# Tile order of one norm, one norm in place, and the order of GpSimd's subtractions in the last expert blocks

## The chip, the cores and the metric

The kernel runs on one core of one Trainium2 chip. The metric is the device time of one execution in microseconds. The engines are named as in the profile: PE (TensorE), DVE (VectorE), ACT (ScalarE), POOL (GpSimd), and SP, whose queue issues the loads.

## The reference

Two networks of two layers each run one after the other on 256 tokens of width 1024 (the first one also carries 256 context tokens as a second sequence). What matters here:

```python
# first network, per layer
h = _ffn_half(h, ...)                       # both sequences
u = _modnorm(h, g, shift, scale)            # h * rsqrt(mean(h*h) + eps) * g, scaled and shifted
y = _fourier_mixer(u, w)                    # layer 0
y, _ = _retention_mixer(u, uc, w_in, ...)   # layer 1: q, k, v, g = split(u @ w_in)
h = h + gate * y
h = _ffn_half(h, ...)
...
x = _rmsnorm(h, final_norm_g)               # ends the first network, is the second one's input

# second network, per layer
u = rmsnorm(x, ln1_w[l]);  proj = u @ w_in[l]   # then three attention branches, merged
x = x + merged @ w_out[l]
x = x + peer_ffn(rmsnorm(x, ln2_w[l]), ...)     # 16384 experts, 128 x 128, gates mostly zero
return rmsnorm(x, lnf_w)
```

In retention q is needed for the 256 tokens of the first sequence only, k and v for both.

## The kernel before

**Layout.** Activations lie by feature: x holds 8 tiles (KD) of 128 features by 512 tokens, the first sequence in columns 0 to 255, the second in 256 to 511. Weights come as a stream of blocks of 1 MB (16 tiles of 128 x 128) through a ring of four slots; SP issues the load of block b when block b-4 is done (`block_done`).

**A product in three parts.** Each weight is split into a rounded part and a rest, and each activation likewise, and PE does rounded x rounded, rounded x rest and rest x rounded. For each half of a block (8 tiles) ACT writes the rounded part into one of two buffers (`round`, line 241; `round_next`, line 3205), and POOL then writes the rest, block minus rounded part, over the ring's slot (`leave_rest`, line 269). A buffer for half h of block b can be rounded again when PE is done with that half of block b-2. PE waits for `rest_done[h]` before half h.

**Stages.** Each engine runs a list of stages in order, each engine with a program of its own; `stage_done` counts finished stages, and finer semaphores join engines inside a stage.

**Norm.** ACT squares the 8 tiles (line 637), PE sums them over features and spreads the inverse root over partitions, DVE scales tiles of 128 x 256 (line 715). Where the next stage multiplies, ACT rounds each scaled tile (line 657) and DVE writes its rest (line 705), which raises `input_split`. With two sequences the 16 tiles come in the order (feature tile 0, sequence 0), (0, 1), (1, 0), ... With `early` set, ACT squares a tile as soon as the stage before has finished it; otherwise it waits for `stage_done`. While the norm runs, ACT also rounds the first two blocks of the next stage.

**Retention** begins with four blocks of 256 columns for q (two halves each, banks 0 to 3, 256 tokens), then k, v, and the gate. Half 0 of block 0 goes along with the norm, tile by tile:

```python
                    if j == 0 and e == 0:
                        self.input_tile(pe, k)     # waits for both sequences' tile k
```

Half 1 of block 0 and blocks 1 to 3 follow. ACT's part of the stage first waits for `stage_done` of the norm, issues a load (line 1257), and then, for each block, rounds the block two ahead (which waits for PE to be done with the present one) and copies q out of PSUM.

**Between the networks** a norm with the final gain writes to another place in SBUF (B_U), and the stage `Replace` copies it into x with one DVE instruction (line 3301). Then the norm of the second network's first layer waits for the whole of it, and ProjectIn follows.

**PeerExperts** runs over 128 expert blocks: 108 in a loop, and 20 "held" ones whose hidden values were worked out earlier. These go in ten pairs, each pair one weight block: half e of block n + p holds the output weights of expert 2p + e. For product (p, e) DVE multiplies the held values by the gates (line 3252), ACT writes the rounded part (line 3192) after PE is done with product (p-1, e), then rounds half e of the pair's next block but for the first one, and DVE writes the rest (line 3254). POOL's order is

```python
        for j in range(n, self.blocks):
            self.leave_rest(j, 0, self.split_count(j))
            self.leave_rest(j - 1, 1, self.split_count(j - 1))
```

while ACT rounds (n+1, 1), (n+2, 0), (n+2, 1), (n+3, 0), ...

Of the kernel before, what the change touches and what calls it, by code (L numbers as in the profile page):

```python
# [16 lines left out]
N = 256  # L17
KD = D // P
# [170 lines left out]
class Stage:  # L189
# [88 lines left out]
    def dve(self, dve, link):  # L278
        pass
# [298 lines left out]
class Norm(Stage):  # L578
# [7 lines left out]
    def __init__(self, chip, out, sq, small, tokens, bank, mod=None, gain=None, parts=None, kept=None, tables=None, mods=None,  # L586
                 lead=None, slots=(4, 5, 6)):
        super().__init__(chip)
# [14 lines left out]
        self.spread = chip.signals("inverse_spread", 1)  # L603
        self.tiles = [(d, s) for d in range(KD) for s in range(tokens // N)]
        self.scaled = chip.signals("scaled", len(self.tiles))
        self.rounded = chip.signals("input_rounded", len(self.tiles) if parts else 0)
        self.input_split = chip.signals("input_split", len(self.tiles) if parts else 0)
# [11 lines left out]
    def act(self, act, link):  # L619
        c, nc = self.chip, self.nc  # L620
        early = isinstance(self.before, (Project, PeerExperts))
        spare = columns(c.vec, "spare")
# [5 lines left out]
        if self.first_mods:  # L628
            lead = self.first_mods
# [104 lines left out]

def first_norm(chip, tokens, mod, mods, split=True, lead=None):
    small = [chip.at(A_SMALL + i * 2 * N, 2 * N)[:, 0:tokens] for i in range(2)]
    sq = chip.at(A_SQ if tokens == 2 * N else R_P, KD, tokens)
    return Norm(chip, chip.at(A_U, KD, 2 * N)[:, :, 0:tokens], sq, small,
                tokens, 7, mod=mod, parts=first_input(chip, tokens) if split else None, mods=mods, lead=lead)

# [309 lines left out]
class Retention(Stage):  # L1050
# [73 lines left out]
    def pe(self, pe):  # L1124
        nc, ps = self.nc, self.chip.ps

        def columns_of(j, out, tokens):

            whi, wlo = self.weights(j)
            for e in range(2):  # L1130
                pe.wait_ge(self.chip.rest_done[e], self.split_count(j))
                for k in range(KD):
                    i = e * KD + k
                    if j == 0 and e == 0:
                        self.input_tile(pe, k)
                    last = self.product(out(e), (whi[:, i, :], wlo[:, i, :]),
                                        (self.u[0][:, k, 0:tokens], self.u[1][:, k, 0:tokens]), k == 0, k == KD - 1)
            last.then_inc(self.chip.block_done, 1)

        for j in range(4):  # L1140
            columns_of(j, lambda e: ps[:, j, e * N:(e + 1) * N], N)
        pe.wait_ge(self.chip.cst1_loaded, 32)

# [1899 lines left out]
class PeerExperts(Stage):  # L3043
# [164 lines left out]
    def pool(self, pool, link):  # L3208
# [5 lines left out]
        with pool.Fori(1, n // RING) as it:  # L3214
            for r in range(RING):
                b = it * RING + r
                self.leave_rest(r, 0, self.split_count(b))
                self.leave_rest((r - 1) % RING, 1, self.split_count(b - 1))
        for j in range(n, self.blocks):
            self.leave_rest(j, 0, self.split_count(j))  # L3220
            self.leave_rest(j - 1, 1, self.split_count(j - 1))
        self.leave_rest(self.blocks - 1, 1, self.split_count(self.blocks - 1))

# [56 lines left out]
def second_network(chip, start):  # L3280
    vec = chip.vec[:]

    stages = [second_norm(chip, columns(vec, "final_g")), Replace(chip)]
    for layer in range(DEPTH):
# [8 lines left out]
    return stages + [final, Finish(chip, final.u)]  # L3293


class Replace(Stage):


    def dve(self, dve, link):
        dve.wait_ge(self.chip.stage_done, self.index)  # L3300
        self.nc.vector.tensor_copy(self.chip.x[:, :, 0:N], self.chip.at(B_U, KD, N)).then_inc(self.chip.stage_done, 1)

# [74 lines left out]
def first_network(chip, start):  # L3377
# [3 lines left out]
    for layer in range(DEPTH):  # L3381
# [4 lines left out]
                               table=dft if first else None)  # L3386
        stages.append(first_norm(chip, 2 * N, 1, mods, split=layer > 0))
        if layer == 0:
# [249 lines left out]
```

## Time and profile before

| | |
|---|---|
| runs | 4486.83, 4493.26 and 4490.0 us; median 4490.0 us |
| profiled execution | 4486.41 us, of which the profile's span is 4484.6 us |
| PE busy | 4287.9 us (96% of the span) |
| POOL busy | 2612.0 us (58%) |
| DVE busy | 1874.5 us (42%) |
| ACT busy | 1863.9 us (42%) |
| mean granted TensorE clock | 0.982 of full speed |

Busy time of PE is no measure of how well it is used, since matmuls are pipelined; the idle times before its instructions and the granted clock tell more. In a timeline a row is: start in us, duration in us, engine, line, operation, what it writes and reads, count, and in brackets the idle time before it with what ended it. Several instructions in a row are merged, with the duration of all of them.

### The profile page before, as it was taken

The numbers are of one execution on the slowest core, as the hardware profiler recorded it, in microseconds if no ns is written. First come the engines' busy times: TensorE is split into PE (matmuls) and PEld (weight loads), VectorE is DVE, ScalarE is ACT, GpSimd is POOL, SyncE is SP. The second block draws the span as 40 slices with busy tenths as digits, with TensorE's granted clock in tenths as the row PEclk, the third lists the DMA queues.
The fourth block names the chain that finished last, engine by engine and source line by source line (L and its number), as shares of the span: only waits on it lengthen the run. The fifth ranks groups of instructions, "written<-read, shape, count | busy, mean of one in ns | idle before, by whom it ended". The sixth has DMA issues, their size and how long they took to land.

```text
span 4484.6 us, 62631 instructions
## 1 busy us (share of the span) xinstructions
PE 4287.9 (96%) x24214; PEld 3670.8 (82%) x24214; DVE 1874.5 (42%) x3572; ACT 1863.9 (42%) x3030; POOL 2612.0 (58%) x1270
## 2 busy tenths in 40 slices
PE   7999999999999999899999999999989999999998
PEld 5787787878878999877897888887868897888886
DVE  5741377032022422554578222223555487222223
ACT  4433343232233444452334555554451424555554
POOL 3443244444444478630467888887720567888886
PEclk9999999999999999999999999999999999999999
DMA  7643367222222245440242455555530351555554
GB/s 264 217 160 94 100 224 273 94 85 99 99 104 94 85 161 187 165 146 34 87 168 71 159 188 187 187 188 207 174 135 20 113 174 39 188 188 188 188 188 160
DMA packets 109503, 659.23 MB, mean 147 GB/s; under 512 B 11504, under 2 KB 17904, under 8 KB 40048
## 3 DMA queue, kind: packets, MB, share of 16 engines
q1 hardware_dynamic: 99072, 637.22, 40.3%
q10 hardware_dynamic: 10224, 19.11, 1.6%
q8 instruction: 148, 2.42, 0.2%
q14 instruction: 59, 0.48, 0.0%
HBM read 646.84 MB, written 9.44 MB: 146 GB/s over the span
## 4 chain that ended last, share of the span: by engine, by line
PE 86%; DVE 6%; ACT 3%; POOL 2%; DMA 1%; issue 1%; SPq 0%; ACTq 0%; DVEq 0%; POOLq 0%
PE ps L3116 15%; PE ps L253 14%; PE ps L255 13%; PE ps L254 13%; PE ps L3106 9%; PE ps L3107 4%; PE ps L3026 3%; PE ps L2822 3%; PE ps L1664 2%; POOL ring_rest L269 2%; DVE arena L2520 1%; ACT rounded L241 1%; PE ps L2189 1%; PE ps L2207 1%; PE ps L1205 1%
## 5 line engine op out<-in xcount | busy, mean ns | idle before, releaser
L269 POOL TENSOR_TENSOR ring_rest<-ring,rounded 128x1024 fp32r<-128x1024 f32 x948 | 2317.6, 2458 | 1324.2 <-ACT rounded L241 1124.3
L253 PE MATMUL ps<-part,rounded 128*128 128x512 f32 (+1 forms) x3360 | 1150.5, 342 | 34.4 <-DVE part L705 21.5
L254 PE MATMUL ps<-part,rounded 128*128 128x512 f32 (+1 forms) x3360 | 1141.7, 340 | 0.0
L255 PE MATMUL ps<-part,ring_rest 128*128 128x512 f32 (+1 forms) x3360 | 1141.4, 340 | 0.0
L241 ACT ACTIVATE rounded<-ring 128x1024 fp32r<-128x1024 f32 x484 | 485.1, 1051 | 651.1 <-PE ps L255 641.5
L253 PEld LDWEIGHTS ps<-part,rounded 128*128 128x128 f32 x3360 | 646.1, 192 | 119.7 <-DVE part L705 21.6
L254 PEld LDWEIGHTS ps<-part,rounded 128*128 128x128 f32 x3360 | 646.5, 192 | 66.9
L255 PEld LDWEIGHTS ps<-part,ring_rest 128*128 128x128 f32 x3360 | 645.6, 192 | 67.4
L3205 ACT ACTIVATE rounded<-ring 128x1024 fp32r<-128x1024 f32 x464 | 490.2, 1056 | 333.0 <-DMA ring<-in_weights 330.8
L3106 PE MATMUL ps<-x_parts,rounded 128*128 128x512 f32 x1728 | 616.9, 397 | 1.5 <-ACTq L3040 1.5
L3116 PE MATMUL ps<-rounded,part 128*128 128x512 f32 x2048 | 592.4, 393 | 16.8 <-POOL ring_rest L269 10.0
L3107 PE MATMUL ps<-x_parts,ring_rest 128*128 128x256 f32 x1728 | 484.7, 280 | 0.0
L3116 PEld LDWEIGHTS ps<-rounded,part 128*128 128x128 f32 x2048 | 369.2, 188 | 99.3 <-POOL ring_rest L269 13.4
L3106 PEld LDWEIGHTS ps<-x_parts,rounded 128*128 128x128 f32 x1728 | 324.7, 188 | 79.4 <-ACTq L3040 1.8
L3236 DVE TENSOR_TENSOR ps<-ps,arena 128x256 f32<-128x256 f32 x216 | 134.8, 624 | 549.4 <-ACT ps L3173 549.4
L3107 PEld LDWEIGHTS ps<-x_parts,ring_rest 128*128 128x128 f32 x1728 | 326.2, 189 | 8.2
L3116 PE MATMUL ps<-ring_rest,part 128*128 128x512 f32 x1024 | 320.7, 395 | 0.0
L443 DVE SCALAR_TENSOR_TENSOR ps<-arena,ps 128x512 f32<-128x512 f32 x392 | 269.2, 746 | 9.1 <-DMA arena<-in_mod_weights 6.9
L3116 PEld LDWEIGHTS ps<-ring_rest,part 128*128 128x128 f32 x1024 | 192.2, 188 | 47.1
L932 DVE SCALAR_TENSOR_TENSOR x<-ps,mods,x 128x256 f32<-128x256 f32 x80 | 35.8, 480 | 456.3 <-PE ps L255 456.3
L821 ACT ACTIVATE arena<-ps 128x512 f32<-128x512 f32 (+1 forms) x88 | 47.9, 544 | 401.5 <-PE ps L255 401.4
L3234 DVE TENSOR_TENSOR ps<-ps,arena 128x256 f32<-128x256 f32 x216 | 93.4, 432 | 240.1 <-ACT arena L3170 240.1
(373 smaller groups left out, 5260.3 us busy)
## 6 DMA issues: line engine op xcount, KB each, us to landing
ring<-in_weights SPq DMA_DIRECT2D x528, 1024.0 KB, 4.8
arena<-in_mod_weights SPq DMA_DIRECT2D x128, 512.0 KB, 4.3
arena<-in_mod_lead SPq DMA_DIRECT2D x8, 1024.0 KB, 18.3
held<-arena ACTq DMA_DIRECT2D x20, 256.0 KB, 5.5
arena<-held SPq DMA_DIRECT2D x20, 256.0 KB, 4.6
arena<-bias_scratch ACTq DMA_DIRECT2D x2, 2048.0 KB, 8.8
bias_scratch<-arena ACTq DMA_DIRECT2D x1, 3072.0 KB, 32.1
x<-in_x SPq DMA_DIRECT2D x1, 2048.0 KB, 9.8
```

The source lines that it names most:

```text
L241: self.nc.scalar.activation(c.rounded[:, s % ROUNDED, half], c.ring[:, slot, half], ACT.Copy)\
L253: mm(out, w[0], a[0], start=start, stop=False)
L254: mm(out, w[0], a[1], start=False, stop=False)
L255: return mm(out, w[1], a[0], start=False, stop=stop)
L269: eng.tensor_tensor(c.ring_rest[:, slot, half], c.ring[:, slot, half], c.rounded[:, (self.s0 + r) % ROUNDED, half].bitcast(F32), ALU.subtr ...
L443: v.scalar_tensor_tensor(bank, self.chunk_row(i, k), self.cond[:, k, stream:stream + 1], bank, ALU.mult, ALU.add)\
L2822: last = nc.tensor.matmul(ps[:, 4 + u % self.AHEAD_BANKS, 0:N], self.chip.ring[:, slot, e * KD + k, :], self.z_whole[:, k, :], start=k == ...
L3106: nc.tensor.matmul(c.ps[:, r % 2, :], whi[:, k, :], c.x_parts[:, k, :], start=k == 0, stop=False)
L3107: last = nc.tensor.matmul(c.ps[:, r % 2, 0:N], wlo[:, k, :], self.z[0][:, k, :], start=False, stop=k == KD - 1)
L3116: last = nc.tensor.matmul(self.out(t, i), a, w[:, i * 4 * P:(i + 1) * 4 * P], start=False, stop=end and n == 2)
L3205: self.nc.scalar.activation(c.rounded[:, (self.s0 + r) % ROUNDED, half], c.ring[:, f % RING, half], ACT.Copy)\
L3236: v.tensor_tensor(gelu, gelu, self.gates[:, :, bass.ds(b + HELD, 1)].rearrange("p t a -> p (t a)"), ALU.mult)\
```

## The change

Three things are changed.

- The norm ahead of retention takes its 16 tiles sequence by sequence (`by_stream`): the 8 tiles of the first sequence, then the 8 of the second. Retention's PE program takes half 0 of blocks 0 and 1 together along with the tiles of the first sequence, then half 1 of block 0 and of block 1, then blocks 2 and 3, and waits for the second sequence's tiles after that.
- The norm at the end of the first network writes into x. `Replace` is gone. The norm after it squares each tile as soon as it is scaled (`x_ready` of a norm is its `scaled` semaphore, and `early` holds for a norm that follows a norm).
- POOL takes the rests of the held blocks in the order in which ACT rounds the halves.

```diff
     def __init__(self, chip, out, sq, small, ..., slots=(4, 5, 6), by_stream=False):
...
         self.tiles = [(d, s) for d in range(KD) for s in range(tokens // N)]
+        if by_stream:
+            self.tiles = [(d, s) for s in range(tokens // N) for d in range(KD)]
         self.scaled = chip.signals("scaled", len(self.tiles))
+        self.x_ready = self.scaled
...
-        early = isinstance(self.before, (Project, PeerExperts))
+        early = isinstance(self.before, (Project, PeerExperts, Norm))
...
-                    if j == 0 and e == 0:
-                        self.input_tile(pe, k)
...
-        for j in range(4):
+        split = self.before.input_split
+
+        def of_query(j, e, k):
+            w, i = self.weights(j), e * KD + k
+            return self.product(ps[:, j, e * N:(e + 1) * N], [x[:, i, :] for x in w], [x[:, k, 0:N] for x in self.u],
+                                k == 0, k == KD - 1)
+
+        for k in range(KD):
+            pe.wait_ge(split.sem, split.at(k + 1))
+            for j in range(2):
+                if k == 0:
+                    pe.wait_ge(self.chip.rest_done[0], self.split_count(j))
+                of_query(j, 0, k)
+        for j in range(2):
+            pe.wait_ge(self.chip.rest_done[1], self.split_count(j))
+            for k in range(KD):
+                last = of_query(j, 1, k)
+            last.then_inc(self.chip.block_done, 1)
+        for j in range(2, 4):
             columns_of(j, lambda e: ps[:, j, e * N:(e + 1) * N], N)
+        pe.wait_ge(split.sem, split.at(2 * KD))
...
-        for j in range(n, self.blocks):
+        for j in (n, n + 1):
             self.leave_rest(j, 0, self.split_count(j))
             self.leave_rest(j - 1, 1, self.split_count(j - 1))
-        self.leave_rest(self.blocks - 1, 1, self.split_count(self.blocks - 1))
+        for j in range(n + 1, self.blocks):
+            self.leave_rest(j, 1, self.split_count(j))
+            if j + 1 < self.blocks:
+                self.leave_rest(j + 1, 0, self.split_count(j + 1))
...
-    stages = [second_norm(chip, columns(vec, "final_g")), Replace(chip)]
+    small = [chip.at(B_SMALL + i * N, N) for i in range(2)]
+    stages = [Norm(chip, chip.x[:, :, 0:N], chip.at(B_SQ, KD, N), small, N, 5, gain=columns(vec, "final_g"))]
...
-class Replace(Stage):
-    def dve(self, dve, link):
-        dve.wait_ge(self.chip.stage_done, self.index)
-        self.nc.vector.tensor_copy(self.chip.x[:, :, 0:N], self.chip.at(B_U, KD, N)).then_inc(self.chip.stage_done, 1)
...
-        stages.append(first_norm(chip, 2 * N, 1, mods, split=layer > 0))
+        stages.append(first_norm(chip, 2 * N, 1, mods, split=layer > 0, by_stream=layer > 0))
```

`first_norm` passes `by_stream` on to `Norm`.

## Rows read from the trace of the kernel before

**Rows 1.** The page, part 4: shares of the chain that ended last, by engine.
```profile
PE 86%; DVE 6%; ACT 3%; POOL 2%; DMA 1%; issue 1%; SPq 0%; ACTq 0%; DVEq 0%; POOLq 0%
```

**Rows 2.** Timeline of PE, held blocks, first and last stall (idle before, releaser in brackets).
```profile
3090.32 0.73 PE L3116 MATMUL ps<-rounded,part 128*128 128x512 f32 x2 [1.26 <-POOL ring_rest L269]
...
4455.35 0.73 PE L3116 MATMUL ps<-rounded,part 128*128 128x512 f32 x2 [1.25 <-POOL ring_rest L269]
```

**Rows 3.** Timeline of ACT, held blocks: three activation copies in a row.
```profile
3086.43 0.38 ACT L3192 ACTIVATE part<-ps 128x256 fp32r<-128x256 f32 x1 [1.39 <-PE ps L3116]
...
3089.15 0.38 ACT L3192 ACTIVATE part<-ps 128x256 fp32r<-128x256 f32 x1 [1.39 <-PE ps L3116]
...
3093.43 0.38 ACT L3192 ACTIVATE part<-ps 128x256 fp32r<-128x256 f32 x1 [2.94 <-PE ps L3116]
```

**Rows 4.** Timeline of POOL, held blocks: rests of halves, two to a row.
```profile
3085.12 5.14 POOL L269 TENSOR_TENSOR ring_rest<-ring,rounded 128x1024 fp32r<-128x1024 f32 x2 [4.06 <-ACT rounded L3205]
3090.56 4.80 POOL L269 TENSOR_TENSOR ring_rest<-ring,rounded 128x1024 fp32r<-128x1024 f32 x2 [0.30 <-ACT rounded L3205]
```

**Rows 5.** Line L269 from 3085 to 3088 us: duration ns min/median/max.
```profile
L269 POOL TENSOR_TENSOR ring_rest<-ring,rounded x2: 2412/2594/2777, 3085.1 to 3087.5; 128x1024 fp32r<-128x1024 f32 x2
```

**Rows 6.** Timeline of DVE, held blocks: a multiply by the gates.
```profile
3087.19 0.84 DVE L3252 TENSOR_TENSOR ps<-arena 128x256 f32<-128x256 f32 x1
```

**Rows 7.** Timeline of DVE, final norm of the first network and what follows.
```profile
1811.73 3.22 DVE L715 SCALAR_TENSOR_TENSOR arena<-x,vec,ps 128x256 f32<-128x256 f32 x8 [0.80 <-PE ps L679]
1815.11 2.47 DVE L3301 COPY x<-arena 128x2048 f32<-128x2048 f32 x1 [0.16 <-DVEq L727]
1821.39 0.43 DVE L693 COPY arena<-ps 128x256 f32<-128x256 f32 x1 [3.82 <-PE ps L670]
```

**Rows 8.** Timeline of ACT, the same stretch.
```profile
1810.72 1.99 ACT L241 ACTIVATE rounded<-ring 128x1024 fp32r<-128x1024 f32 x2
1817.61 2.56 ACT L637 ACTIVATE arena<-x 128x256 f32<-128x256 f32 x8 [4.91 <-DVE x L3301]
```

**Rows 9.** Timeline of all engines, the same norm of the second layer.
```profile
3145.43 2.54 ACT L637 ACTIVATE arena<-x 128x256 f32<-128x256 f32 x8
...
3148.76 0.42 DVE L693 COPY arena<-ps 128x256 f32<-128x256 f32 x1 [3.37 <-PE ps L670]
```

**Rows 10.** Timeline of PE at the start of ProjectIn after the final norm.
```profile
1825.44 0.58 PE L253 MATMUL ps<-part,rounded 128*128 128x256 f32 x1 [1.69 <-DVE part L705]
```

**Rows 11.** Windows there: us, PE, PEld, DVE, ACT, POOL busy (instructions), granted clock, DMA.
```profile
1831.00:1831.50 0.50, 0.50 (x4) 0.50 (x4) 0.50 (x1) 0.00 (x0) 0.00 (x0) 0.52 1.07 389
```

**Rows 12.** Timeline of DVE, norm of retention: the first and the last rests.
```profile
1278.23 0.48 DVE L705 SCALAR_TENSOR_TENSOR part<-ps,mods,part 128x256 fp32r<-128x256 f32 x1
...
1290.07 1.26 DVE L705 SCALAR_TENSOR_TENSOR part<-ps,mods,part 128x256 fp32r<-128x256 f32 x3
```

**Rows 13.** Timeline of PE, first matmul of retention and two later ones.
```profile
1279.76 0.55 PE L253 MATMUL ps<-part,rounded 128*128 128x256 f32 x1 [2.75 <-DVE part L705]
...
1293.05 0.41 PE L254 MATMUL ps<-part,rounded 128*128 128x256 f32 x1
1293.26 0.41 PE L255 MATMUL ps<-part,ring_rest 128*128 128x256 f32 x1
```

**Rows 14.** Timeline of ACT, start of retention.
```profile
1291.42 0.34 ACTq L1257 DMA_DIRECT2D arena<-in_expo  x1
1296.82 2.01 ACT L241 ACTIVATE rounded<-ring 128x1024 fp32r<-128x1024 f32 x2 [6.15 <-PE ps L255]
...
1302.58 2.01 ACT L241 ACTIVATE rounded<-ring 128x1024 fp32r<-128x1024 f32 x2 [3.27 <-PE ps L255]
```

**Rows 15.** Timeline of POOL, norm and start of retention.
```profile
1276.61 2.35 POOL L269 TENSOR_TENSOR ring_rest<-ring,rounded 128x1024 fp32r<-128x1024 f32 x1 [0.96 <-ACT rounded L241]
1297.96 4.76 POOL L269 TENSOR_TENSOR ring_rest<-ring,rounded 128x1024 fp32r<-128x1024 f32 x2 [19.00 <-ACT rounded L241]
```

**Rows 16.** Windows of the retention stage, columns as in rows 11.
```profile
1292.00:1296.00 4.00, 4.00 (x22) 4.00 (x22) 0.00 (x0) 0.00 (x0) 0.00 (x0) 0.55 0.73 262
```

More of the change, by code:

```diff
@@ L586, in __init__ @@
     def __init__(self, chip, out, sq, small, tokens, bank, mod=None, gain=None, parts=None, kept=None, tables=None, mods=None,
-                 lead=None, slots=(4, 5, 6)):
+                 lead=None, slots=(4, 5, 6), by_stream=False):
         super().__init__(chip)
@@ L732, in first_input, with first_norm @@
     return tuple(chip.parts_at(a, KD, 2 * N)[:, :, 0:tokens] for a in (A_SQ, A_U))
-def first_norm(chip, tokens, mod, mods, split=True, lead=None):
+def first_norm(chip, tokens, mod, mods, split=True, lead=None, by_stream=False):
     small = [chip.at(A_SMALL + i * 2 * N, 2 * N)[:, 0:tokens] for i in range(2)]
@@ L738, in first_norm @@
     return Norm(chip, chip.at(A_U, KD, 2 * N)[:, :, 0:tokens], sq, small,
-                tokens, 7, mod=mod, parts=first_input(chip, tokens) if split else None, mods=mods, lead=lead)
+                tokens, 7, mod=mod, parts=first_input(chip, tokens) if split else None, mods=mods, lead=lead, by_stream=by_stream)
 class FeedForwardIn(Stage):
```

## The prediction

> **What bounds the kernel now.** I read the shares of the chain first: 86% of it is PE, so time is won only where PE stands still or runs at its lower clock [rows 1]. The change touches three places, so next came the timelines of PE, ACT, POOL and DVE there, for what ends PE's wait in each.
>
> *Held blocks* (end of each PeerExperts). A product here is PE's work on half a block, 12 matmuls. ACT's copy for a product starts when PE has finished the product two earlier, so the distance of copies is PE's pace: 3086.43 to 3089.15 is 2.72 us, and the next one 4.28 us [rows 3]. The difference, 1.56 us, is a stall of PE that POOL's rest ends; there are four in each layer, and of the eight in both the first and the last are shown [rows 2]. POOL itself is not full: it stood idle for 4.06 us before the rest that PE then waited behind, and that pair of rests ended at 3090.26, just as PE went on [rows 2, 4].
>
> *Final norm of the first network.* PE has nothing but the norms. Eight scaled tiles take 3.22 us on DVE, then comes a copy of 2.47 us, and only then eight squares on ACT; the next norm's sums are copied at 1821.39 [rows 7, 8].
>
> *Start of retention.* PE waits 2.75 us for its first tile, then does three matmuls for each two tiles of the norm, at half clock [rows 13]. The norm's last rest ends at 1290.07 + 1.26 = 1291.33 [rows 12]; the granted clock from 1292 to 1296 is 0.55, so it was 1.2 GHz until about 1295.6 and 2.4 GHz then [rows 16]. ACT rounds block 2 at 1296.82, when block 0 is done, and block 3 at 1302.58, when block 1 is done [rows 14].
>
> **Part 1, held blocks.** POOL's instructions are the same; two of each pair change places. Before, the rest of (p+1, half 0) went ahead of that of (p, half 1); but (p+1, 0) can be rounded only after PE has finished (p-1, 0), while (p, 1) was rounded earlier. POOL so stood waiting with work at hand, and PE got (p, 1) a whole rest late. After, POOL takes halves in the order in which ACT rounds them.
>
> What is late next? Take a product done at 0. ACT's copy takes 0.38, the rounding one half of 1.99, about 1.0, so POOL can begin near 1.4 [rows 3, 8]. A rest takes 2.41 to 2.78 [rows 5], so it is there by 4.3. PE needs that half as the fourth product from there, after three more: 3 x 2.72 = 8.2. That leaves 3.9 us. POOL at its slowest, 2.78 for each product against 2.72, falls behind by 0.06 x 18 = 1.1 us in a layer, less than 3.9. So no stall stays: 8 x 1.56 = 12.5 us. The lower bound lets the 1.1 us through in both layers: 10.3. I take 12.5, since the reserve is over three times the slip.
>
> The two rests of that pair differ, 2.41 and 2.78, and a DVE multiply by the gates (both inputs in SBUF), from 3087.19 to 3088.03, lies across the point where one ends and the next begins [rows 5, 6]. The Trainium skill, "SBUF — State Buffer", section "Who interferes with whom", says that a DVE instruction with two SBUF inputs and a GpSimd instruction that reads SBUF lock each other out for a whole instruction. This speaks against the change, as closer-packed rests meet every multiply: by the rule, and with the 2.78 that the trace has for a rest that met one, the 12.5 would become at worst the 10.3 above.
>
> **Part 2, final norm.** Replace and its copy go; DVE writes the scaled tiles straight into x, and the next norm's squares wait for each tile instead of the whole stage. The tiles end at 1811.73 + 3.22 = 1814.95, the last square follows after 0.03 and takes about 0.42 (2.56 for eight overlapping ones): 1815.40. ACT is no bound: it is free of rounding at 1810.72 + 1.99 = 1812.71, and eight squares from there end at 1815.27 [rows 7, 8]. From the last square to the copy of the sums is 1821.39 - (1817.61 + 2.56) = 1.22 us in the present norm; in the second layer's, where squares already follow tiles, it is 3148.76 - (3145.43 + 2.54) = 0.79 us [rows 7 to 9]. So the copy starts at 1816.19 or 1816.62, not at 1821.39: 5.2 or 4.8 us. I take 5.2, as that norm has the new shape. Nothing is queued behind the new waits of ACT but its rounding of the next block, which PE needs about 4 us later. ProjectIn then runs at half clock from 1825.44 to about 1831.3 [rows 10, 11]. This stretch may shorten: at half clock a matmul takes 0.21 instead of 0.12 us (below), so each us of it costs 0.43 us. Half of it gone would add 1.3; I put 0 and keep 1.3 for the range.
>
> **Part 3, retention.** The order of tiles costs DVE and ACT nothing: the same 16 tiles, 0.91 us each. A full block of q is 48 matmuls in 5.76 us, the distance of the roundings at 1296.82 and 1302.58: 0.12 us each; at half clock 0.21 [rows 13, 14]. The first tile's rest ends at 1278.23 + 0.48 = 1278.71 [rows 12], and PE now starts there, with six matmuls for each tile. They take 1.28 us at half clock, more than the 0.91 of a tile, so PE is dense from the start and I expect the clock back within a few us; then it follows the tiles, and the first halves of blocks 0 and 1 are done at about 1278.7 + 8 x 0.91 = 1286.0. Both second halves follow without waiting, as the last rest of block 1 ends at 1276.61 + 2.35 = 1278.96 [rows 15]: 48 x 0.12 more, blocks 0 and 1 done at about 1291.7 instead of 1302.5.
>
> Not all of these 10.8 us stay. ACT rounds block 2 only behind its wait for the whole norm. That wait still ends near 1291.42, then comes the issue of the expo load, and rounding can start at 1291.8. POOL starts 1.14 later (1296.82 to 1297.96) and a rest is half of 4.76 [rows 14, 15]: 1292.9 + 2.4 = 1295.3, and PE starts block 2 at 1295.4. So the gain is 1302.5 - 1295.4 = 7.1 us, whether blocks 0 and 1 end at 1291.7 or 3 us later. Blocks 3 and on are not late: POOL then does a rest each 2.4 us, PE uses one each 2.9.
>
> PE now stands still for 3.7 us, where before it didn't. After its wait of 2.75 us ahead of the first tile the clock was at 1.2 GHz [rows 13], so I expect that again. It costs the dense stretch at half clock: from 1291.4 to 1295.6 here, 4.2 us x 0.43 = 1.8; from 1825.44 to 1831.3, 5.9 x 0.43 = 2.5 [rows 10, 11, 16]. I take 1.8: 5.3 us stay, bounds 4.6 and 7.1, and 3.5 if PE keeps half clock all through blocks 0 and 1 (96 x 0.21 from 1278.7 is 1299).
>
> The Trainium skill, "TensorE: Matmul & The Clock Gate", section "Why this matters for your kernels", advises against idle gaps between bursts of matmuls, since the engine falls back to its lower clock. By this rule the change loses part of what it wins, 5.3 instead of 7.1, and the trace agrees with it at 1279.76.
>
> **The sum.** 12.5 + 5.2 + 5.3 = 23.0 us. The profiled execution took 4486.4 (span 4484.6 and 1.8 around it): 4463.4. The median of the three runs is 4490.0, 3.6 above it, so I say **4467**. The terms' bounds give 10.3 + 4.8 + 3.5 = 18.6 to 12.5 + 6.5 + 7.1 = 26.1, so 4464 to 4471 on the median's scale; the runs shown spread by 3.3 either way, and the likeliest case's own range is 4460 to 4475. About 0.2%, 9 us, can be told from no change.
>
> **Rivals.**
> *Held blocks keep their pace.* If POOL waits for a rounding ahead of each rest, as it does for 0.30 us ahead of some now [rows 4], a product costs 2.78 + 0.30 = 3.08; two pairs are then 12.3, against 3 x 2.72 + 4.28 = 12.4 now, and nothing is won there: 4490 - 10.5 = 4479.5. Against it: 2.78 is the slow one of the rests, and the reserve of 3.9 us has to be used up first. 0.09; half of it counts as no change, being 0.23% off.
> *Retention wins nothing*, because the gap ahead of block 2 and a clock that stays low through blocks 2 and 3 (a further 7 us) take it all: 4490 - 17.7 = 4472.3. Against it: the clock came back within 6 us of dense work in both places seen. 0.08.
> *No change to be told*: weight loads, not PE, set the pace once PE is early, and the three gains end in waits for them: 4486 to 4490. Against it: in the held blocks ACT's copies wait for PE, none for a load [rows 3]. 0.07.
> *Slower*: the held half that POOL now takes first is rounded after PE's product of that half, not before, so that each product waits for copy, rounding and rest, 4.3 us, less one product of 2.72: 1.6 us x 36 = 57, less 10.5, is 4490 + 46 = 4536. It decides once the lead of a rest falls from 8.2 to under 4.0 us (0.28 us for each product eats the other 10.5). The copies being released two products ahead speaks against it [rows 3]. 0.04.
>
> The forecast itself has 0.72. Faster: 0.72 + 0.08 + 0.05 = 0.85; no change 0.07 + 0.04 = 0.11; slower 0.04. With the first two cases, 4459 to 4477 holds about 8 in 10.
>
> **What would show it.** Held blocks: ACT's copies 2.72 us apart all through, PE with no wait for POOL. Final norm: one copy fewer on DVE, and about 4.5 us from the first scaled tile to the copy of the next sums instead of 9.7. Retention: PE starts about 1 us earlier, ends blocks 0 and 1 near the norm's last rest, then waits over 3 us for POOL's first rest of block 2, and the clock falls once more. I would be wrong if rests still end PE's waits in the held blocks, if ACT can't round block 2 by 1292, or if a later stage waits for something that didn't become earlier.

## The result

The changed kernel takes 4461.06 us (median of 4 runs, 4456.06 to 4461.67), the kernel before 4489.65 beside it (4 runs, 4486.83 to 4493.26): a ratio of 0.9934, 95% interval 0.9918 to 0.995. That is faster, by 28.6 us, and clear of the noise, where 23.0 were forecast (4467; range 4459 to 4477). The profiled executions have spans of 4484.6 and 4459.4, 25.2 us apart.

The shares of the chain, in part 4 of the profile's page of the kernel after, stand against [rows 1]: POOL has lost a point, PE and DMA have gained one each.

```profile
PE 87%; DVE 6%; ACT 3%; DMA 2%; issue 1%; POOL 1%; SPq 0%; ACTq 0%; DVEq 0%; POOLq 0%
```

**Held blocks.** PE's waits between 3050 and 3135 us of the kernel after, from the view of waits (us in total, times, longest):

```profile
PE ps L3136 <- DVE part L3262: 2.3, 1, 2.3
PE ps L673 <- ACT arena L640: 1.7, 1, 1.7
PE ps L3175 <- ACT arena L3218: 0.7, 1, 0.7
```

From its timelines of ACT, POOL and DVE, copies in a row, rests and a multiply:

```profile
3087.00 0.39 ACT L3212 ACTIVATE part<-ps 128x256 fp32r<-128x256 f32 x1 [1.39 <-PE ps L3136]
...
3089.72 0.39 ACT L3212 ACTIVATE part<-ps 128x256 fp32r<-128x256 f32 x1 [1.39 <-PE ps L3136]
...
3092.44 0.39 ACT L3212 ACTIVATE part<-ps 128x256 fp32r<-128x256 f32 x1 [1.38 <-PE ps L3136]
...
3074.81 2.40 POOL L269 TENSOR_TENSOR ring_rest<-ring,rounded 128x1024 fp32r<-128x1024 f32 x1 [2.80 <-ACT rounded L3225]
...
3088.41 2.57 POOL L269 TENSOR_TENSOR ring_rest<-ring,rounded 128x1024 fp32r<-128x1024 f32 x1 [0.20 <-ACT rounded L3225]
3091.13 30.07 POOL L269 TENSOR_TENSOR ring_rest<-ring,rounded 128x1024 fp32r<-128x1024 f32 x11 [0.16 <-ACT rounded L3225]
...
3087.76 0.95 DVE L3275 TENSOR_TENSOR ps<-arena 128x256 f32<-128x256 f32 x1
```

No line of the waits names POOL, nor does one in the second layer, where POOL ended four of PE's waits in each layer before, the first and the last of them in [rows 2] (the 2.3 us stand at the entry of these blocks, as before). From the third copy on, the copies are 2.72 us apart, where [rows 3] has 4.28 in between. POOL begins with rests of 2.40 us and idles a little before each; each rest then is longer than the one before it, and from 3091.13 on eleven stand back to back in 30.07 us, 2.73 each, just over PE's 2.72. POOL is full there now. The multiply above takes 0.95 us, where [rows 6] has 0.84, and each one is a little longer than the one before it, from 0.82 to 1.29 us in this layer.

**Final norm.** Timelines of DVE, ACT and PE of the kernel after:

```profile
1812.78 3.22 DVE L718 SCALAR_TENSOR_TENSOR x<-x,vec,ps 128x256 f32<-128x256 f32 x8 [0.80 <-PE ps L682]
1817.23 0.42 DVE L696 COPY arena<-ps 128x256 f32<-128x256 f32 x1 [1.23 <-PE ps L673]
...
1813.66 2.79 ACT L640 ACTIVATE arena<-x 128x256 f32<-128x256 f32 x8
...
1830.29 2.01 ACT L241 ACTIVATE rounded<-ring 128x1024 fp32r<-128x1024 f32 x2 [4.73 <-PE ps L255]
...
1821.27 0.39 PE L253 MATMUL ps<-part,rounded 128*128 128x256 f32 x1 [1.69 <-DVE part L708]
```

The same rounding of ACT in the kernel before:

```profile
1837.10 2.01 ACT L241 ACTIVATE rounded<-ring 128x1024 fp32r<-128x1024 f32 x2 [7.38 <-PE ps L255]
```

Windows of the kernel after there (columns as in [rows 11]):

```profile
1821.00:1823.00 2.00, 1.73 (x14) 1.73 (x15) 1.90 (x6) 1.06 (x3) 1.21 (x1) 1.00 0.00 0
1825.00:1827.00 2.00, 2.00 (x19) 2.00 (x18) 1.84 (x5) 0.39 (x1) 0.00 (x0) 1.00 0.40 99
```

The squares start 0.88 us behind the first scaled tile, with no copy between, and from that tile to the copy of the sums it is 4.45 us, where [rows 7] has 9.66: 5.2 us less. And the clock is 1.00 when ProjectIn starts, so that the first matmul takes 0.39 us where [rows 10] has 0.58. PE's first two blocks there, up to ACT's next rounding, take 9.02 us (1821.27 to 1830.29) against 11.66 (1825.44 to 1837.10): another 2.6 us.

**Retention.** Timelines of DVE, ACT, POOL and PE of the kernel after:

```profile
1294.92 1.26 DVE L708 SCALAR_TENSOR_TENSOR part<-ps,mods,part 128x256 fp32r<-128x256 f32 x3
...
1296.27 0.34 ACTq L1277 DMA_DIRECT2D arena<-in_expo  x1
1296.71 2.00 ACT L241 ACTIVATE rounded<-ring 128x1024 fp32r<-128x1024 f32 x2 [1.19 <-DVEq L727]
...
1297.84 2.35 POOL L269 TENSOR_TENSOR ring_rest<-ring,rounded 128x1024 fp32r<-128x1024 f32 x1 [14.05 <-ACT rounded L241]
...
1283.60 0.58 PE L253 MATMUL ps<-part,rounded 128*128 128x256 f32 x1 [1.75 <-DVE part L708]
...
1300.25 0.40 PE L253 MATMUL ps<-part,rounded 128*128 128x256 f32 x1 [3.46 <-POOL ring_rest L269]
```

Its windows there:

```profile
1284.00:1286.00 2.00, 2.00 (x11) 2.00 (x11) 1.93 (x6) 1.03 (x3) 0.00 (x0) 0.50 0.01 4
1288.00:1292.00 4.00, 4.00 (x36) 4.00 (x35) 3.82 (x10) 2.12 (x5) 0.00 (x0) 1.00 0.00 0
...
1300.90:1302.90 2.00, 2.00 (x11) 2.00 (x11) 0.00 (x0) 0.67 (x2) 2.00 (x2) 0.50 1.04 438
```

Everything here is 4.8 us later than before by the trace, since the start of this profile was. Less that, PE's first tile comes 1.0 us earlier than in [rows 13], the last rest of the norm is where [rows 12] has it, and ACT rounds block 2 at 1296.71, not at 1296.82 + 4.8 = 1301.6 [rows 14]. PE has blocks 0 and 1 done by then, stands still for 3.46 us until POOL's first rest of block 2 is there, and the clock, back at 1.00 by 1288, falls to 0.50 a second time.

A ledger over the whole run: how much later the same ScalarE instruction starts in each profile than in the profile of before (us from the span's start). The last column is a second profile of the kernel after.

| at us of before | what lies between | after | retention alone | norm alone | held alone | after, again |
|---|---|---|---|---|---|---|
| 1269 | start of the program | +4.83 | +7.31 | +5.12 | +5.46 | +3.60 |
| 1350 | retention's start | -0.47 | +2.91 | +5.18 | +5.28 | -1.72 |
| 1805 | rest of the first layer | +1.05 | +4.46 | +5.16 | +5.29 | -3.21 |
| 1838 | final norm, two blocks of ProjectIn | -6.81 | +3.05 | -2.71 | +5.11 | -11.09 |
| 1965 | | -8.75 | +4.51 | -4.96 | +1.07 | -13.42 |
| 3041 | | -8.98 | +4.71 | -5.18 | +6.55 | -13.14 |
| 3145 | held blocks, first layer | -13.78 | +4.81 | -3.66 | +2.03 | -19.41 |
| 3293 | | -18.89 | +4.71 | -8.37 | +1.89 | -23.56 |
| 4302 | | -18.77 | +4.88 | -8.28 | +1.84 | -23.56 |
| 4476 | held blocks, second layer | -25.24 | +4.53 | -8.46 | -4.52 | -28.53 |

Each edit takes its time off at its own place: 5.3 us at retention's start, 7.9 between 1805 and 1838, and in each layer's held blocks 6.2, since from the third of ACT's twenty copies to the eighteenth it is 46.99 us before (3083.71 to 3130.70) and 40.80 after (3076.12 to 3116.92). That makes 25.6 us with both layers. A row of the table can hold a half-clock stretch besides: 4.8 for the first layer of the kernel after, as the clock was at 0.57 from 3068 to 3072 there; 4.4 for retention alone, as the clock fell one pause of PE earlier there and the norm's first tile came 0.9 us later. The rows without an edit move by up to 5.5 us either way; the experiment on the clock's falls is about them. The first row is no loss of the change: the profile of before reaches 1269 earlier than all thirteen others, by 1.5 to 7.3 us, which is one reason why the spans differ by less than the medians.

### The profile page after: what moved, and what is told of

Same layout as the page of the kernel before. It is cut to its first block, busy times and chain, and to the rows that moved or that the text cites. A ratio compares the mean times of both kernels' runs of the same rounds, so it can differ in the third digit from the quotient of the medians.

```text
span 4459.4 us, 62630 instructions
## 1 busy us (share of the span) xinstructions
PE 4280.7 (96%) x24214; PEld 3667.2 (82%) x24214; DVE 1883.1 (42%) x3571; ACT 1864.8 (42%) x3030; POOL 2618.6 (59%) x1270
## 4 chain that ended last, share of the span: by engine, by line
PE 87%; DVE 6%; ACT 3%; DMA 2%; issue 1%; POOL 1%; SPq 0%; ACTq 0%; DVEq 0%; POOLq 0%
PE ps L3136 16%; PE ps L253 13%; PE ps L255 13%; PE ps L254 13%; PE ps L3126 9%; PE ps L3127 4%; PE ps L3046 3%; PE ps L2842 3%; PE ps L1684 2%; DVE arena L2540 1%; PE ps L2209 1%; ACT rounded L241 1%; PE ps L2227 1%; POOL ring_rest L269 1%; DMA ring<-in_weights 1%
## 5 line engine op out<-in xcount | busy, mean ns | idle before, releaser
L269 POOL TENSOR_TENSOR ring_rest<-ring,rounded 128x1024 fp32r<-128x1024 f32 x948 | 2323.7, 2466 | 1300.8 <-ACT rounded L241 1119.2
```

The costliest lines, as they stand in the source:

```text
L269: eng.tensor_tensor(c.ring_rest[:, slot, half], c.ring[:, slot, half], c.rounded[:, (self.s0 + r) % ROUNDED, half].bitcast(F32), ALU.subtr ...
```

## Experiments

**The parts one by one.** Each is the kernel before with one part of the change as it stands in the diff. *Retention alone*:

```diff
-        stages.append(first_norm(chip, 2 * N, 1, mods, split=layer > 0))
+        stages.append(first_norm(chip, 2 * N, 1, mods, split=layer > 0, by_stream=layer > 0))
...
+            for j in range(2):
...
+                of_query(j, 0, k)
```

> The kernel before with the retention part alone (norm by sequence, first two q blocks together). My theory: blocks 0 and 1 end about 10 us earlier, 3.5 us of it go to PE's wait for POOL's rest of block 2 and about 1.7 to the clock that falls in that wait, so 5.3 us stay: 4489.65 - 5.3 = 4484. From the norm's copy of sums (1273.49 before) to the end of block 3 (ACT's rounding at 1314.10 before, 40.6 us) 35.3 us. Rival (the unexplained 3 us of the whole change come from this part): 4481. Rival (the gain is given back later in the stage): 4489.

Measured: 4486.89 us against 4491.53 for the kernel before, ratio 0.9989 (0.998 to 0.9998). From the copy of sums to ACT's rounding at the end of block 3 it is 36.2 us, not 35.3, by the 0.9 us that the earlier fall of the clock cost.

*Final norm alone*:

```diff
-        early = isinstance(self.before, (Project, PeerExperts))
+        early = isinstance(self.before, (Project, PeerExperts, Norm))
...
-    stages = [second_norm(chip, columns(vec, "final_g")), Replace(chip)]
+    stages = [Norm(chip, chip.x[:, :, 0:N], chip.at(B_SQ, KD, N), small, N, 5, gain=columns(vec, "final_g"))]
```

> The kernel before with the final norm in place, Replace gone, squares per tile. My theory: from the first scaled tile to the copy of the next sums 4.45 us instead of 9.66, so 5.2 us for certain, and up to 2.6 more where ProjectIn starts at 2.4 GHz, as in the changed kernel: 4482 to 4484.5. If the clock at the start of ProjectIn belongs to the shorter idle stretch, the granted clock there is 1.0 again; the rival, that it was chance, lets it be 0.5 for some us, with 5.2 us or less won.

Measured: 4480.25, ratio 0.9975 (0.9966 to 0.9984). The clock is 1.00 again where ProjectIn starts.

*Held blocks alone*:

```diff
-        for j in range(n, self.blocks):
+        for j in (n, n + 1):
             self.leave_rest(j, 0, self.split_count(j))
             self.leave_rest(j - 1, 1, self.split_count(j - 1))
+        for j in range(n + 1, self.blocks):
+            self.leave_rest(j, 1, self.split_count(j))
+            if j + 1 < self.blocks:
+                self.leave_rest(j + 1, 0, self.split_count(j + 1))
```

> The kernel before with POOL's order in the held blocks alone. My theory: eight stalls of 1.56 us go, ACT's copies are 2.72 us apart all through, POOL's rests grow to about 2.7 us but PE never waits for them: 4489.65 - 12.4 = 4477.2. Rival (closer-packed rests are held up by the multiplies): stalls stay late in each layer, 4479.5 or more.

Measured: 4477.66, ratio 0.9966 (0.9954 to 0.9978). The copies are 2.72 us apart from the third on, in both layers.

*All three together*, beside them:

> The changed kernel once more, for a second profile. My theory: the three parts add up to 12.4 + 5.3 + 7.8 = 25.5 us, 4464; what is beyond (the median fell by 28.6) comes from stretches of lower clock elsewhere that lie differently in each execution, so a second profile has them in other places and the same three gains at the three places. Rival: the same places outside the change (around 1940 and 3270 us) are shorter by 2 to 3 us again, so that the change reaches them.

Measured: 4461.77, ratio 0.9934 (0.9921 to 0.9948). The three medians are 4.6, 11.3 and 13.9 us below before, 29.8 in all, and the whole is 29.8: the parts add up, with no sign that they hide or feed one another, though each interval is 4 us or more either way, so that the exact agreement is luck. At their places they won 4.4, 7.9 and 12.4 us. The norm's median has 3.4 us more than that. The profile of all three together has the gains at the same places (5.3, 7.9, and 6.1 and 6.4 in the two layers' rows), and around 1940 and 3270 it is again about 4 us shorter each, which is the sign that the rival named; more on that below.

**What gave ProjectIn its clock.** The kernel before, with the copy gone but the squares still behind the whole of the final norm, not tile by tile:

```diff
-    stages = [second_norm(chip, columns(vec, "final_g")), Replace(chip)]
+    stages = [Norm(chip, chip.x[:, :, 0:N], chip.at(B_SQ, KD, N), small, N, 5, gain=columns(vec, "final_g"))]
```

> The kernel before, with one half of the edit at the first network's final norm: the norm writes its result in place and the copy stage goes, but the squares are still formed behind the last residual sum, not block by block ahead of it. Theory (the 2.6 us that the change won in ProjectIn beyond my sum are the clock's: it keeps full only if PE's idle time ahead of ProjectIn is short enough): the copy's 2.5 us are won, and the clock in ProjectIn still falls to half as before, since PE's gap is only 2.5 us shorter: 4487 against 4489.65. Rival: the 2.6 us come with any shorter gap: 5 us less than before, 4484.5.

At the same place of this kernel, the timeline of ACT:

```profile
1819.93 2.56 ACT L637 ACTIVATE arena<-x 128x256 f32<-128x256 f32 x8 [2.33 <-DVEq L727]
```

The view of waits, for PE:

```profile
PE ps L670 <- ACT arena L637: 3.8, 1, 3.8
```

And windows:

```profile
1820.00:1822.00 2.00, 1.60 (x10) 0.98 (x12) 0.00 (x0) 2.00 (x7) 1.39 (x1) 0.50 0.00 0
1828.00:1830.00 2.00, 1.33 (x6) 1.34 (x7) 1.93 (x6) 1.08 (x3) 0.87 (x1) 0.50 0.00 0
```

Measured: 4483.6 against 4492.67, ratio 0.998 (0.9971 to 0.9989). The trace bears out the theory: at its place the edit won 2.6 us from the norm to ACT's rounding in ProjectIn (+4.89 to +2.31 in the ledger's measure), the copy's time and no more, and the clock was at 0.50 when ProjectIn started. (The next norm's sums are copied 2.6 us earlier; its other steps, at half clock here, take 0.9 longer, and ProjectIn's two blocks 0.9 less.) PE's idle time ahead of the squares' sums was 6.4 us before, is 3.8 here and 1.4 after. Over the 14 profiles of this study, the first matmul of ProjectIn ran at half clock in all four without early squares, and in one of the ten with them (the kernel with the early rounding, below: 0.50; in one more, the one with an extra multiply of two SBUF operands, the clock fell 1 us behind the first matmul). The median fell by 9.1 us, so 6.5 came from elsewhere; of these 4.0 us stand in its trace at 1937 to 1960 us, and they are taken up below.

**What is left in retention.** After, with block 2 rounded among the norm's tiles:

```diff
+        self.ahead = (12, 13) if by_stream else None
...
+                if self.ahead and i in self.ahead:
+                    self.next.round(act, ROUNDED, halves=(self.ahead.index(i),))
...
-            self.round(act, j + ROUNDED)
+            if j:
+                self.round(act, j + ROUNDED)
```

> The kernel after, with one thing moved: ScalarE rounds the two halves of retention block 2 among its normalized tiles (after tiles 12 and 13) and not behind the whole norm. Theory: what is left of the wait in this stage is PE's 3.5 us for GpSimd's first rest of block 2, because the rounding begins only at 1296.71, behind the last tile; begun some 2 us earlier the rest comes earlier by as much, PE waits about 1 us, and the granted clock does not fall a second time there: 2.5 to 4 us less than after, about 4457.5. Rival: the two roundings push the last three normalized tiles of ScalarE back by their 4 us, the rests of those tiles and PE's first blocks come as much later, and nothing is won: 4461, or 1 to 2 us more.

And with another order of PE's first two blocks as well (both halves of block 0 with the tiles, then block 1; rounding after tiles 10 and 11):

```diff
-            for j in range(2):
+            for e in range(2):
...
-                    pe.wait_ge(self.chip.rest_done[0], self.split_count(j))
-                of_query(j, 0, k)
+                    pe.wait_ge(self.chip.rest_done[e], self.split_count(0))
+                last = first_queries(0, e, k)
+        last.then_inc(self.chip.block_done, 1)
...
+                last = first_queries(1, e, k)
```

> The kernel after, with block 2 rounded among the tiles (after tiles 10 and 11) and PE's two blocks in another order: both halves of block 0 run with the tiles as they come, block 1 as a whole follows. Then PE has a whole block of finished operands to work on while GpSimd makes the rest of block 2. Theory (the wait for GpSimd's rest is all that is left here): the 3.5 us wait goes, and with it the clock's second fall, together 4 to 5 us less than after, about 4456. Rival: the wait only moves to block 3's rest, which GpSimd makes next, or PE's start waits for the tiles that the roundings delay: within 2 us of after, 4459 to 4463.

PE's waits in this stage that a rest of POOL ends, from the view of waits, with the early rounding:

```profile
PE ps L253 <- POOL ring_rest L269: 0.8, 1, 0.8
```

All of PE's waits in the stage with both edits, from the same view:

```profile
PE ps L253 <- DVE part L711: 1.8, 1, 1.8
PE ps L681 <- DVE arena L699: 0.9, 1, 0.9
PE ps L685 <- DVE arena L701: 0.6, 1, 0.6
```

And a window of it where the kernel after had the clock at 0.50:

```profile
1301.00:1303.00 2.00, 2.00 (x19) 2.00 (x18) 0.00 (x0) 1.01 (x2) 1.63 (x1) 1.00 0.95 291
```

Measured: 4460.12 us with the early rounding (ratio to before 0.9924, 0.9911 to 0.9937) and 4455.75 with both (0.9916, 0.9903 to 0.9929). From PE's first tile to the rounding of block 4 (24.26 us in the kernel after) the traces show 21.34 and 20.29: 2.9 and 4.0 us less. The wait shrank to 0.8 us and then went, and the clock stayed at 1.00 both times (1.00 in every window from 1291 to 1303 with the early rounding). The median of the first is only 0.9 us below the 4461.06 of the kernel after, which was not run beside it, so its 2.9 us rest on the trace; in its profile ProjectIn started at half clock and lost 2.6 us there. The second once more, beside the kernel after:

> The kernel in which both halves of retention's block 0 run with the tiles and block 2 is rounded among them, once more and now beside the kernel after. Theory: 4.0 us less than after, the difference of the two traces in this stage: 4457 against 4461. Rival: nothing is won in the end, since the clock's stretches further on give it back: 4461.

Measured: 4455.89 (ratio 0.9916, 0.9903 to 0.993) and the kernel after 4459.46 (0.9931, 0.9916 to 0.9946). That is 3.6 us less by medians. In this second profile the same stretch takes 19.12 us, 5.1 less than after, as the clock came back almost 3 us earlier than in the first one. The intervals overlap, so the gain rests on the 4.0 and 5.1 us of the two traces and on the median being lowest both times; it is the fastest kernel here.

**POOL's rests and DVE's multiplies.** After, with each held multiply done twice (the extra result goes to a spare tile):

```diff
+            v.tensor_tensor(self.low[:, e, :], h, self.gates[:, :, n], ALU.mult)
             v.tensor_tensor(self.hidden(e), h, self.gates[:, :, n], ALU.mult).then_inc(self.gated.sem, 1)
```

> The kernel after, with VectorE's multiply of a held block done twice (the first result is overwritten in place): one more operation with two SBUF inputs for each of the 18 blocks of a layer. VectorE itself has room for it. Theory: GpSimd's rest of a held block and VectorE's two-input multiply do not run side by side in full (the rests grow from 2.40 to 2.73 us where multiplies fall into them), so each rest grows by another 0.5 to 1.0 us past ScalarE's 2.72 us, GpSimd becomes the bound again, and the run takes 8 to 12 us per layer more, 17 to 24 us in all: about 4481. Rival: the rests grow for another reason (the narrow slack of their order), and the extra multiply costs nothing: 4461.

Timelines of DVE and POOL of this kernel:

```profile
3100.14 0.61 DVE L3275 TENSOR_TENSOR arena<-arena 128x256 f32<-128x256 f32 x1
...
3102.07 1.95 DVE L3275 TENSOR_TENSOR arena<-arena 128x256 f32<-128x256 f32 x1
3103.95 2.79 DVE L3276 TENSOR_TENSOR ps<-arena 128x256 f32<-128x256 f32 x1
...
3100.79 5.49 POOL L269 TENSOR_TENSOR ring_rest<-ring,rounded 128x1024 fp32r<-128x1024 f32 x2 [1.90 <-ACT rounded L3225]
```

Measured: 4497.13 against 4492.67 (ratio 1.0005, 0.9997 to 1.0014): the whole gain is gone, 36 us above the 4461 of the kernel after (32 by the two ratios to before) where 17 to 24 were expected. The direction was the theory's, but not the way in which the time is lost. Alone, at 3100.14, the multiply takes 0.61 us. Two rests stand from 3100.79 to 3106.28 and meet near 3103.53; the multiplies issued under them end at 3104.02 and 3106.74, each 0.5 us behind the end of a rest. A rest takes 2.75, hardly more than the 2.73 of the kernel after. It is DVE that waits out the whole rest, ACT's copy waits for DVE, and PE and POOL for that: the copies are 1.93 and 5.46 us apart in turn, so a product takes 3.7 us on average instead of 2.72.

Whether that is the operands or only the place of the extra work, two more kernels tell: the extra multiply in DVE's idle time behind the real one, once with both operands in SBUF and once with one in PSUM.

```diff
             v.tensor_tensor(self.hidden(e), h, self.gates[:, :, n], ALU.mult).then_inc(self.gated.sem, 1)
+            v.tensor_tensor(self.low[:, e, :], h, self.gates[:, :, n], ALU.mult)
```

> The kernel after, with one more multiply of two SBUF operands on VectorE for each held block, written to a spare tile, in VectorE's idle 1.4 us between the multiply and ScalarE's copy. Theory: such an operation waits until GpSimd's rest under way has ended and takes 0.47 us from there, so it reaches 1.3 us past the start of the subtraction behind it, and then the next block's multiply runs into the next rest: at least the 36 us of the doubled multiply, up to one whole rest per block (18 x 2.75 us in each layer, 99 us): 4497 to 4560. Rival: what cost 36 us was the extra work ahead of the multiply in VectorE's order and not its operands; put into idle time it costs nothing: 4461, and the same as the next kernel.

```diff
+            v.tensor_tensor(self.low[:, e, :], c.ps[:, e, 0:N], self.gates[:, :, n], ALU.mult)
```

> The same extra multiply at the same place, but with its first operand read from PSUM, so that only one of the two is in SBUF. Theory (two SBUF operands are what excludes GpSimd): it takes some 0.5 to 0.6 us in VectorE's idle time, GpSimd's rests stay at 2.73 us or less, and the time stays that of after: 4459 to 4465. Rival (any VectorE operation that reads or writes SBUF excludes GpSimd): the same loss as with two SBUF operands, 4497 or more.

Groups by line of the held blocks (behind the first bar the busy time and the mean ns); L3276 is the extra multiply. With two SBUF operands:

```profile
L269 POOL TENSOR_TENSOR ring_rest<-ring,rounded 128x1024 fp32r<-128x1024 f32 x17 | 46.6, 2767 | 12.4 <-ACT rounded L3225 12.4
...
L3275 DVE TENSOR_TENSOR ps<-arena 128x256 f32<-128x256 f32 x17 | 29.7, 1749 | 0.0
...
L3276 DVE TENSOR_TENSOR arena<-arena 128x256 f32<-128x256 f32 x18 | 24.2, 1344 | 0.0
```

With one operand in PSUM:

```profile
L269 POOL TENSOR_TENSOR ring_rest<-ring,rounded 128x1024 fp32r<-128x1024 f32 x17 | 46.4, 2770 | 1.9 <-ACT rounded L3225 1.9
...
L3275 DVE TENSOR_TENSOR ps<-arena 128x256 f32<-128x256 f32 x19 | 31.0, 1631 | 0.0
...
L3276 DVE TENSOR_TENSOR arena<-ps,arena 128x256 f32<-128x256 f32 x19 | 11.5, 607 | 0.0
```

Measured: 4481.87 with two SBUF operands, 4461.9 with one in PSUM, 4459.46 for the kernel after beside them. So the operands decide: the PSUM form takes 0.61 us each time, though POOL's rests run nearly without a break; the SBUF form takes 1.34 on average, 0.61 for twelve of the eighteen and 2.8 for the other six. The loss of 22 us is less than the 36 I gave as the least: I had let every block lose a rest, while POOL is idle for 12.4 us above, waiting for rounded halves, and the twelve short multiplies all began while no rest was under way.

The Trainium skill, "SBUF — State Buffer", section "Who interferes with whom", has this as a rule: a VectorE instruction with two SBUF inputs and a GpSimd instruction that reads SBUF exclude each other for a whole instruction, the one issued first holding off the other, while one with at most one SBUF input, outside the modes that use two ports, does not. The traces agree: 2.79 us against 0.61 for the same multiply.

**The clock's falls.** The kernel after once more:

> The kernel after once more, beside the three others of this call on one chip: 4461 us, as in its two earlier timings. Its profile also shows which of the half-clock stretches of TensorE come again in the same places (theory: those at 1541, 1908 and 3270 follow from the program and come again; rival: they come and go with each execution).

Windows at the same instructions, each behind PE's row at the end of the pause ahead of it, from its timeline: first the kernel after, at 1541.5 us:

```profile
1541.41 2.00 PE L1245 MATMUL ps<-arena,cst 128*128 128x256 f32 x7 [1.88 <-ACT arena L1330]
...
1541.50:1545.50 4.00, 4.00 (x17) 3.67 (x18) 1.43 (x2) 3.99 (x5) 0.44 (x1) 0.67 0.54 227
```

Its second profile, at 1540.25:

```profile
1540.16 1.99 PE L1245 MATMUL ps<-arena,cst 128*128 128x256 f32 x8 [1.88 <-ACT arena L1330]
...
1540.25:1544.25 4.00, 4.00 (x27) 3.79 (x28) 1.42 (x2) 3.99 (x5) 0.43 (x1) 1.00 0.51 217
```

The kernel before, at 1934:

```profile
1933.56 2.17 PE L2091 MATMUL ps<-arena,ring 64*128 64x256 f32 x5 [1.68 <-ACT arena L2273]
...
1934.00:1938.00 4.00, 4.00 (x15) 3.35 (x14) 0.00 (x0) 0.95 (x3) 0.00 (x0) 0.50 0.52 213
```

The kernel with the held blocks alone, whose edit comes later than this, at 1939.1:

```profile
1938.67 1.31 PE L2091 MATMUL ps<-arena,ring 64*128 64x256 f32 x5 [1.68 <-ACT arena L2273]
...
1939.10:1943.10 4.00, 4.00 (x23) 3.31 (x22) 0.73 (x2) 2.43 (x7) 0.00 (x0) 1.00 0.53 221
```

Measured: 4459.46 us. Mixed: the fall at 1541 did not come again; that named as 1908 (at 1894.5 us of the first profile) did, with 1.6 us lost in both; and around 3270 both have the same short stretch. So the rival holds at 1541, and the second pair of windows shows the same elsewhere. Ahead of the first pair PE paused for 1.88 us in both profiles, ahead of the second for 1.68 in both, and behind the same pause the clock was 0.67 in one and 1.00 in the other, 0.50 and 1.00. Such a fall costs 1.3 us at 1541 and about 4 around 1940 and 3270 each. Falls of this kind move the ledger's other rows: where one of them grows or shrinks by over 1 us, the time at half clock in it does so too.

Around 3270, again the kernel before, and the kernel after at the same instructions:

```profile
3262.00:3266.00 4.00, 4.00 (x14) 3.08 (x13) 0.00 (x0) 1.48 (x4) 0.00 (x0) 0.50 0.39 164
3247.14:3251.14 4.00, 4.00 (x26) 3.04 (x24) 1.11 (x3) 2.81 (x8) 0.00 (x0) 1.00 0.43 182
```

That does not mean that the edits have no part in it. Over the 14 profiles the 4 us around 3270 were lost in all four without early squares and in two of the ten with them (the early rounding and the PSUM operand), those around 1940 in two of the four and none of the ten. The smaller falls became more frequent: the one named 1908 is in one of the four and eight of the ten, and that at 1541, ahead of the norm's edit, in none of the four without retention's edit and eight of the ten with it. By these few counts the change is worth 3.2 + 2.0 - 0.9 - 1.0 = 3.3 us on average at places that it doesn't touch. That is an estimate, and how an edit reaches so far on is not shown.

## Why the prediction was right

**Held blocks: right in mechanism and size.** 12.4 us for 12.5: four stalls in each layer are gone and the copies keep 2.72. The slip by the slow rests was there as named, 2.73 us for each product, and the reserve of 3.9 us held it. The lower bound of 10.3 was not needed, and the rival in which the pace stays was wrong because POOL needs no idle time before each rest (eleven in 30.07 us). That the multiplies would meet every rest came true; it cost nothing, as a rest with its multiply, 2.73 us, is hardly longer than PE's 2.72.

**Final norm: the mis-sized term.** The norm itself gave 5.2 us, as forecast. For ProjectIn's start at half clock I put 0, with 1.3 as the bound (half of that stretch gone); all of it went, 2.6 us, twice the bound. The step that failed is "ProjectIn then runs at half clock": with 1.4 us of idle PE ahead of the squares' sums instead of 6.4, the clock did not fall in eight of ten profiles. In the kernel with the early rounding, where ProjectIn started at half clock, the part was worth 5.3 us from norm to rounding, the forecast's number. The price of half clock, 0.43 us for each us, was right: the 0.52 of [rows 11] puts the stretch's end near 1831.5, so it is 6.0 us long, and it came to 2.6. Some of the 2.6 is luck: ProjectIn's first two blocks took 10.3 to 11.7 us in the four profiles without early squares, and the profile of before has the longest, against 9.0 in the eight.

**Retention: right, step by step.** Blocks 0 and 1 were done near the norm's last rest, the rounding began at 1296.71 (1291.8 + 4.8 forecast), POOL 1.13 us behind it (1.14), PE waited for 3.46 us (3.7), and the clock fell a second time; 5.3 us stay of 7.1. The kernel without the wait and the fall won 4.0 and 5.1 us more in its two profiles. None of the rivals on record came about.

The Trainium skill, "TensorE: Matmul & The Clock Gate", section "Why this matters for your kernels", warns of idle gaps of PE; the trace agrees at the 3.46 us gap here, but the falls behind 1.68 and 1.88 us show that shorter gaps can cost too, in one execution and not in the next.

**The sum.** 23.0 were forecast, 25.6 were won at the three places, and 28.6 by medians. The first 2.6 are the clock in ProjectIn. The last 3.0 have no term in the prediction: it named no gain outside the three places. The falls at other places differ between executions by that much, and by the counts above (3.3 us) they would come from the norm's edit, but that is an estimate and no experiment: around 1940 (the second pair of windows) the clock also stayed up in one kernel without any edit to the norm, held blocks alone. The terms' own bounds ended at 26.1 us, 4464; that 4461 lies within the stated range is owed to the room left for scatter between runs, not to a term.

## What to carry to other kernels

Let an engine take its operands in the order in which the engine before it finishes them: a strict interleave that looks even can leave ready work waiting behind one late item. When a gap of PE is closed, count the clock of the dense stretch behind it as well as the gap, here at 0.43 us for each us at half clock. And before VectorE is given work beside GpSimd, look whether both its operands lie in SBUF: with one in PSUM, the extra multiplies here cost nothing that could be measured (4461.9 against 4459.46).

## What was not expected of the hardware

The same instructions, behind the same pause of PE, run at full clock in one execution and at half in another (1.88 us: 1.00 and 0.67; 1.68 us: 1.00 and 0.50), so that one profile's ledger is uncertain by some 4 to 5 us at a place. And a multiply of 0.61 us can take 2.79 beside a GpSimd rest of 2.75, ending about 0.5 us behind it: nearly all of the waiting is done by the multiply, and the rest itself shows only 0.4 us of it (2.35 to 2.75).
